# One matrix product over high and low activations together, in the feed-forward layers of a two-block transformer kernel

## The chip, the cores and the metric

The kernel runs on one core of one Trainium2 chip. The metric is the device time of one execution in microseconds (us): 1653.76 us, the median of three runs (1652.23 to 1656.18).

TensorE (PE in the profile) multiplies matrices and writes to PSUM, which here is two tensors of four banks, `psw` and `psa`, each bank 128 partitions x 512 fp32 values. VectorE (DVE), ScalarE (ACT) and GpSimd (POOL) work on SBUF and PSUM; SyncE (SP) issues the loads. Each engine runs its own instruction list in order, and waits on semaphores for the others.

## The reference

Two blocks, each of two layers (`L = 2`), act on 256 tokens of width 1024 in fp32. What bears on the change are the four feed-forward layers, with an inner width of 2816. Block 1:

```python
g, u = jnp.split(x @ w_gu, 2, axis=-1)
ffn = (jax.nn.silu(g) * u) @ w_down
ple = (p_i @ w_pp) * jax.nn.sigmoid(x @ w_pg)
return layer_norm(DN_ALPHA * x + ffn + ple, ln2_g, ln2_b)
```

Block 2 puts a causal convolution of three taps over the tokens between the product and the gate:

```python
u = x @ w_up
u = lax.conv_general_dilated(u, conv_w[:, None, :], padding=[(CONV_W - 1, 0)], ...) + conv_b
a, g = jnp.split(u, 2, axis=-1)
return (a * jax.nn.silu(g)) @ w_down
```

Around them stand the attentions, the norms and the other projections, which the change does not touch.

## The kernel before, in words

**Products in three parts.** TensorE takes fp32r operands here. To keep the precision of fp32, each weight tile (128 x 2048 values, 1 MB) is split: ScalarE rounds it to its high part `whi` (`split`, L1179), VectorE subtracts that from the original and has the low part `wlo` (L1515). Activations are split in the same way into `xhi` and `xlo`. `product` (L687) then adds three matrix products into one bank: high x high, high x low, low x high. Low x low is dropped.

**A feed-forward layer** is cut into `FS = 11` steps of 256 inner columns. A step has a gate tile `g` and an up tile `u` (`by_features`, L737: two halves of 128 features, in each 8 values of k, in each three matmuls over 256 tokens), then a down tile `d` of an earlier step (`down`, 24 matmuls of 512 columns into `psa`). `down_steps(s)` gives which: step s runs the down tile s-1 for s = 1 to 8, none in step 9, tile 8 in step 10, and behind the steps tiles 9 and 10 interleaved by token half and column half. The gate tile of a step fills bank 0 or 2 of `psw` and the up tile bank 1 or 3, alternately, so that two steps' results can stand at once.

**What follows a tile.** In block 1, ScalarE takes silu of the gate bank (L1380), and VectorE multiplies by the up bank (L1916), rounds (L1921) and subtracts (L1923): the two parts of `hidden(s)`, released by `hid_ready`. In block 2, ScalarE first makes the middle tap and the bias of the convolution from the bank (L1488, two instructions a tile), VectorE adds the other two taps (L2103, eight instructions a step), ScalarE takes silu (L1494), and VectorE multiplies (L2113), rounds (L2119) and subtracts (L2121).

**Order of the splits.** Weights move through rings: five raw tiles and five low tiles, three high tiles. `serve(key)` on ScalarE and VectorE issues the splits for which the tile `key` makes room; a high part can be made once the tile three places before it in the ring is done. So the tile done first makes room for one that is needed two tiles later. Where `serve` stands among the other instructions of ScalarE and VectorE sets which goes first. SP loads a raw tile when the tile five places before it is done.

**Block 1's per-layer gate.** The four banks of `x @ w_pg` go through exp (ScalarE, L1370) and, on VectorE, +1, reciprocal (L1898) and a product with `ple` (L1901), in the order of the loop at L1892. All of it stands ahead of step 0. TensorE waits for all four exps (`pg_exp`, L976) before step 0. In step 2 `ple` is added to `xtok` (L1933).

Of the kernel before, what the change touches and what calls it, by code (L numbers as in the profile page):

```python
# [9 lines left out]
F32R = mybir.dt.float32r  # L10
I32 = mybir.dt.int32
ALU = mybir.AluOpType
# [3 lines left out]
P = 128  # L16
# [188 lines left out]
def build(nc, w, c, out):  # L205
# [41 lines left out]
    with ExitStack() as ctx:  # L247
# [16 lines left out]
        xhi = sb("xhi", [KD, S], F32R)  # L264
        xlo = sb("xlo", [KD, S], F32R)
# [154 lines left out]
        xpT_ready = sem("xpT_ready")  # L420
        conv_first = sem("conv_first")
# [52 lines left out]
        conv_g = r1[:, 2560:3584].rearrange("p (b c s) -> p b c s", b=2, c=2)  # L474
        gact = r1[:, 512:1536].rearrange("p (b c) -> p b c", b=2)
# [205 lines left out]
        def _(pe):  # L681
# [67 lines left out]

            def norm_turns(key, t, src=xtok):  # L750
# [93 lines left out]
            def ffn(block, l, f0, norm_key, behind_up=lambda: None):  # L844
# [38 lines left out]
            for l in range(L):  # L883
# [92 lines left out]
                pe.wait_ge(pg_exp, 4 * (l + 1))  # L976

                def next_p():
                    pe.wait_ge(hid_ready, FS * (l + 1) - 1)
                    p_turns(l + 1, 2 * ((l + 1) * FS % 2))  # L980
                if l + 1 < L:
                    ffn(1, l, FS * l, None, next_p)
                else:
                    ffn(1, l, FS * l, None)
# [186 lines left out]
        def _(act):  # L1171
# [62 lines left out]

            def p_high(l, bank):
# [65 lines left out]
            for l in range(L):  # L1301
# [71 lines left out]
                for s in range(FS + 1):  # L1373
                    f = FS * l + s
                    if s < FS:
                        serve((1, "g", l, s))
                        if f >= 2:
                            act.wait_ge(hid_ready, f - 1)
                        act.wait_ge(tile_done, ti[(1, "g", l, s)] + 1)
                        nc.scalar.activation(gact[:, f % 2, :], psw[:, 2 * (f % 2), :],  # L1380
                                             ACT.Silu).then_inc(gate_ready, 1)
                        serve((1, "u", l, s))
                    if s == FS - 1 and l + 1 < L:
                        p_high(l + 1, 2 * ((l + 1) * FS % 2))
# [6 lines left out]
            for l in range(L):  # L1391
# [85 lines left out]
                for s in range(FS + 1):  # L1477
                    f = FS * (L + l) + s
                    if s < FS:
                        for name, buf, bank, ch0 in (("g", conv_g, 2 * (f % 2), 22 + 2 * s),  # L1480
# [748 lines left out]
```

## Time and profile before

| | |
|---|---|
| median of three runs | 1653.76 us |
| the profiled execution | 1651.49 us, its span 1649.7 us |
| PE busy | 1531.9 us (93%), 9781 matmuls |
| DVE busy | 1055.8 us (64%) |
| ACT busy | 716.0 us (43%) |
| mean granted TensorE clock | 0.966 of full |

Busy time of a matmul is a modelled duration, and neighbours overlap: how fast TensorE goes is read from the distance of the starts in a timeline. A group's mean duration is therefore longer than the time that one of its matmuls takes in a row of them. The idle time named in a group is that of its engine just before it, with what ended it. A wait for several semaphores is put down to the one that came last.

### The profile page before, as it was taken

To read this page: it belongs to the slowest core of one execution; us is meant where nothing else is said; L and a number is where in the kernel's file an instruction comes from. 1 tells how busy PE (TensorE), PEld (TensorE's weight loads), DVE (VectorE), ACT (ScalarE), POOL (GpSimd) and SP (SyncE) were. 2 spreads that over 40 slices of the span, in tenths; PEclk is the share of its full clock that TensorE was granted. 3 is DMA by queue.
4 is the path that set the end of the run, shared out by engine and by line. 5 is a ranking of instruction groups with operands and counts; after the bars stand their busy time and mean duration, and the time that the engine had idled before them with its cause. 6 is when DMAs were issued, how large, how long until landed. Compare 5 with 4: busy or idle time off the path is not lost.

```text
span 1649.7 us, 24186 instructions
## 1 busy us (share of the span) xinstructions
PE 1531.9 (93%) x9781; PEld 1365.4 (83%) x9781; DVE 1055.8 (64%) x1676; ACT 716.0 (43%) x1042; POOL 61.9 (4%) x58
## 2 busy tenths in 40 slices
PE   6799999999989999979999889999899998899997
PEld 5677899998777999968877769999788777799996
DVE  6786955567869664575365456677853664566766
ACT  4355333334553333424464343545444652435442
POOL 0100000000100000011000000000010000000000
PEclk9899999999999999989999999999999998899998
DMA  8533555655434655634433623556445346335551
GB/s 294 180 128 111 177 179 190 213 182 182 138 113 147 224 193 179 232 126 127 155 118 117 222 100 132 188 194 205 154 126 156 117 134 205 101 130 188 194 179 51
DMA packets 184690, 267.26 MB, mean 162 GB/s; under 512 B 7382, under 2 KB 139396, under 8 KB 184452
## 3 DMA queue, kind: packets, MB, share of 16 engines
q1 hardware_dynamic: 179684, 260.48, 47.9%
q10 hardware_dynamic: 4896, 5.25, 0.9%
q8 instruction: 78, 1.28, 0.3%
q14 instruction: 32, 0.26, 0.0%
HBM read 260.46 MB, written 5.24 MB: 161 GB/s over the span
## 4 chain that ended last, share of the span: by engine, by line
PE 71%; DVE 15%; ACT 4%; DVEq 4%; issue 3%; POOL 2%; DMA 1%; SPq 0%; ACTq 0%; POOLq 0%
PE psw L689 16%; PE psw L691 16%; PE psw L690 16%; PE psa L689 4%; PE psa L690 4%; PE psa L691 4%; DVE wlo L1515 3%; POOL rstd L2148 2%; PE psa L778 2%; PE psa L781 2%; DVE xtok L1547 1%; DVE sy L1603 1%; DVE r L1898 1%; DVEq L1607 1%; PE psw L799 1%
## 5 line engine op out<-in xcount | busy, mean ns | idle before, releaser
L1515 DVE TENSOR_TENSOR wlo<-raw,whi 128x2048 fp32r<-128x2048 f32 (+2 forms) x201 | 452.9, 2259 | 318.3 <-ACT whi L1179 318.0
L1179 ACT ACTIVATE whi<-raw 128x2048 fp32r<-128x2048 f32 (+2 forms) x201 | 379.5, 1890 | 338.6 <-PE psw L691 247.3
L689 PE MATMUL psw<-xhi,whi 128*128 128x256 f32 x1472 | 416.8, 283 | 2.6 <-ACT r L1370 1.4
L691 PE MATMUL psw<-xhi,wlo 128*128 128x256 f32 x1472 | 416.6, 283 | 0.0
L690 PE MATMUL psw<-xlo,whi 128*128 128x256 f32 x1472 | 416.5, 283 | 0.0
L689 PEld LDWEIGHTS psw<-xhi,whi 128*128 128x128 f32 x1472 | 282.4, 192 | 5.1 <-ACT r L1370 2.2
L690 PEld LDWEIGHTS psw<-xlo,whi 128*128 128x128 f32 x1472 | 282.4, 192 | 1.2
L691 PEld LDWEIGHTS psw<-xhi,wlo 128*128 128x128 f32 x1472 | 282.5, 192 | 0.0
L689 PE MATMUL psw<-whi,xhi 128*128 128x512 f32 (+3 forms) x472 | 184.9, 392 | 16.9 <-DVE wlo L1515 13.8
L691 PE MATMUL psw<-whi,xlo 128*128 128x512 f32 (+3 forms) x472 | 181.4, 384 | 0.0
L690 PE MATMUL psw<-wlo,xhi 128*128 128x512 f32 (+3 forms) x472 | 181.4, 384 | 0.0
L689 PE MATMUL psa<-whi,rr 128*128 128x512 f32 x352 | 139.1, 395 | 5.4 <-DVE wlo L1515 5.4
L690 PE MATMUL psa<-wlo,rr 128*128 128x512 f32 x352 | 138.4, 393 | 0.0
L691 PE MATMUL psa<-whi,rr 128*128 128x512 f32 x320 | 124.5, 389 | 0.0
L689 PEld LDWEIGHTS psw<-whi,xhi 128*128 128x128 f32 x472 | 90.8, 192 | 35.2 <-DVE wlo L1515 15.6
L1488 ACT ACTIVATE r<-psw,pcol 128x256 f32<-128x256 f32 x88 | 45.0, 562 | 146.0 <-PE psw L691 146.0
L2103 DVE SCALAR_TENSOR_TENSOR r<-psw,pcol,r 128x255 f32<-128x255 f32 (+1 forms) x176 | 72.8, 476 | 54.3 <-ACT r L1488 52.7
L691 PEld LDWEIGHTS psw<-whi,xlo 128*128 128x128 f32 x472 | 90.5, 192 | 16.3
L690 PEld LDWEIGHTS psw<-wlo,xhi 128*128 128x128 f32 x472 | 90.8, 192 | 15.3
L1267 ACT ACTIVATE sy<-sy,nmx 128x256 f32<-128x256 f32 (+1 forms) x160 | 70.6, 443 | 54.6 <-DVE nmx L1616 54.6
L2148 POOL TENSOR_TENSOR rstd<-vare,mhalf 128x1 f32<-128x1 f32 x26 | 38.6, 1484 | 1459.2 <-DVE vare L1537 1459.2
L689 PEld LDWEIGHTS psa<-whi,rr 128*128 128x128 f32 x352 | 67.0, 190 | 19.2 <-issue 6.2
(261 smaller groups left out, 1944.2 us busy)
## 6 DMA issues: line engine op xcount, KB each, us to landing
raw<-in_w_gu SPq DMA_DIRECT2D x44, 1024.0 KB, 5.1
raw<-in_ffn_w_up SPq DMA_DIRECT2D x42, 1024.0 KB, 5.1
raw<-in_w_down SPq DMA_DIRECT2D x22, 1024.0 KB, 4.9
raw<-in_ffn_w_down SPq DMA_DIRECT2D x22, 1024.0 KB, 4.9
raw<-in_w_in SPq DMA_DIRECT2D x20, 1024.0 KB, 5.4
raw<-in_xa_wkv SPq DMA_DIRECT2D x16, 1024.0 KB, 5.5
raw<-in_w_o SPq DMA_DIRECT2D x8, 1024.0 KB, 5.1
raw<-in_w_out SPq DMA_DIRECT2D x8, 1024.0 KB, 5.3
```

The costliest lines, as they stand in the source:

```text
L689: pe.matmul(o, lh, rh, start=first, stop=False)
L690: pe.matmul(o, lh, rl, start=False, stop=False)
L691: return pe.matmul(o, ll, rh, start=False, stop=last)
L778: ins = pe.matmul(psa[:, 3, 0:TC], weight[:, k, piece], memT[:, k, :], start=k == 0, stop=k == KD - 1)
L781: ins = pe.matmul(psa[:, 3, 0:TC], memT[:, k, piece], weight[:, k, :], start=k == 0, stop=k == KD - 1)
L799: ins = pe.matmul(psw[:, 2 * (i % 2) + a, b * S:b * S + nk], qT(kind, h, t), kT(kind, h, nk), start=True, stop=True)
L1179: nc.scalar.activation(tile_flat("hi", i), tile_flat("raw", i), ACT.Copy).then_inc(hi_ready, 1)
L1267: ins = nc.scalar.activation(soft[:, u % 2, h, 0:nk], soft[:, u % 2, h, 0:nk], ACT.Exp, bias=nmx[:, u % 2, h:h + 1], scale=1.0, accum_out= ...
L1488: ins = nc.scalar.activation(buf[:, f % 2, ch, :], bank2(psw, bank)[:, ch, :], ACT.Identity, scale=pcol[:, 2 + 2 * l, cc:cc + 1], bias=pco ...
L1515: v.tensor_tensor(tile_flat("lo", i), tile_flat("raw", i), tile_flat("hi", i).bitcast(F32), ALU.subtract).then_inc(lo_ready, 1)
L2103: ins = v.scalar_tensor_tensor(out=o, in0=bank2(psw, bank)[:, ch, 0:S - lag], scalar=pcol[:, j, cc:cc + 1], in1=o, op0=ALU.mult, op1=ALU.add)
L2148: g.tensor_tensor(rstd[:, t:t + 1], vare[:, t:t + 1], mhalf[:, t:t + 1], ALU.pow).then_inc(ln_rstd, 1)
```

## The change

Four things are done together.

1. `xhi` and `xlo` become the two halves of one buffer `xboth`. For the gate and up tiles `by_features_wide` replaces `by_features`: for each k, one matmul takes the high weights against both halves at once (512 columns: columns 0 to 255 of the bank get high x high, 256 to 511 high x low) and one takes the low weights against `xhi` (256 columns, into the first half). A half tile of 128 features now fills a whole bank; the gate tile uses banks 0 and 1, the up tile banks 2 and 3, in every step.
2. The two halves of a bank have to be added: `ffn_low` (ScalarE) copies the second halves to SBUF, `ffn_sum` (VectorE) adds the first halves and writes `gsum` or `usum` in SBUF. silu, the products and the convolution read these in place of PSUM. TensorE waits for `ffn_summed` of the step before, bank pair by bank pair, where it waited for `hid_ready` of two steps before.
3. VectorE's order: in block 2 the taps are made for the gate tile and the up tile apart; in both blocks the product and its rounding go ahead of the splits that the up tile releases. At the end of a feed-forward layer TensorE runs both column halves of down tile 9 and then both of tile 10, for each token half.
4. Block 1's gates (+1, reciprocal, product) are spread over steps 1 to 4, `ple` is added in step 5, and TensorE waits bank by bank for the exps.

```diff
-        xhi = sb("xhi", [KD, S], F32R)
-        xlo = sb("xlo", [KD, S], F32R)
+        xboth = sb("xboth", [2, KD, S], F32R)
+        xhi, xlo = xboth[:, 0], xboth[:, 1]
...
+            def by_features_wide(key, bank0, free, ready=None):
+                wh, wl = take(key)
+                for ch in range(TC // P):
+                    bank = psw[:, bank0 + ch, :]
+                    cols = slice(ch * P, (ch + 1) * P)
+                    free(bank0 + ch)
+                    for k in range(KD):
+                        if ready is not None and ch == 0:
+                            turns_ready(ready, NT - 1, k)
+                        if k:
+                            pe.matmul(bank[:, 0:S], wl[:, k, cols], xhi[:, k, :], start=False, stop=False)
+                        ins = pe.matmul(bank.rearrange("p (i s) -> p i s", i=2), wh[:, k, cols], xboth[:, :, k, :],
+                                        start=k == 0, stop=k == KD - 1)
+                        if k == 0:
+                            pe.matmul(bank[:, 0:S], wl[:, k, cols], xhi[:, k, :], start=False, stop=False)
+                ins.then_inc(tile_done, 1)
...
-                    if f >= 2:
-                        pe.wait_ge(hid_ready, f - 1)
-                    by_features((block, "g", l, s), bank2(psw, 2 * (f % 2)), xhi, xlo,
-                                norm_key if s == 0 else None)
-                    by_features((block, "u", l, s), bank2(psw, 2 * (f % 2) + 1), xhi, xlo)
+                    def gate_free(bank):
+                        if s:
+                            pe.wait_ge(ffn_summed, 2 * f - 1)
+                        else:
+                            first_free(bank)
+                    def up_free(bank):
+                        if s:
+                            pe.wait_ge(ffn_summed, 2 * f)
+                        else:
+                            first_free(bank)
+                    by_features_wide((block, "g", l, s), 0, gate_free, norm_key if s == 0 else None)
+                    by_features_wide((block, "u", l, s), 2, up_free)
...
                     for half in range(2):
                         ins = down(FS - 2, t, half)
-                        if t == 1 and half == 1:
-                            ins.then_inc(tile_done, 1)
+                    if t == 1:
+                        ins.then_inc(tile_done, 1)
+                    for half in range(2):
                         ins = down(FS - 1, t, half)
...
-                pe.wait_ge(pg_exp, 4 * (l + 1))
+                def gate_read(bank):
+                    pe.wait_ge(pg_exp, 4 * l + (1, 3, 2, 4)[bank])
...
+            def ffn_low(block, l, s, i):
+                act.wait_ge(tile_done, ti[(block, "gu"[i], l, s)] + 1)
+                nc.scalar.activation(low_part[:, i], psw[:, 2 * i:2 * i + 2, S:2 * S], ACT.Copy).then_inc(low_out, 1)
...
+            def ffn_sum(block, l, s, i):
+                dve.wait_ge(low_out, 2 * (FS * (l + L * (block - 1)) + s) + i + 1)
+                v.tensor_tensor((gsum, usum)[i].rearrange("p (c s) -> p c s", c=2), psw[:, 2 * i:2 * i + 2, 0:S],
+                                low_part[:, i], ALU.add).then_inc(ffn_summed, 1)
...
+                        ffn_sum(2, l, s, 0)
+                        taps(l, s, 0, conv_g, gsum, 22 + 2 * s).then_inc(conv_done, 1)
                         serve((2, "g", l, s))
-
-                        dve.wait_ge(conv_first, 2 * (FS * l + s + 1))
...
-                        if s < FS - 1:
-                            serve((2, "u", l, s))
+                        ffn_sum(2, l, s, 1)
+                        taps(l, s, 1, conv_a, usum, 2 * s)
                         dve.wait_ge(gate_ready, f + 1)
...
-                    if s == FS - 1:
+                    if s < FS:
                         serve((2, "u", l, s))
```

VectorE in one step of block 2's first layer (step 7 of 11), before. `r<-psw,pcol,r` are taps, `wlo` a split, `r<-r 128x512` the product, the two `rr` rows the two parts of the hidden tile.

```order
L2103 SCALAR_TENSOR_TENSOR r<-psw,pcol,r 128x255 x4
L2103 SCALAR_TENSOR_TENSOR r<-psw,pcol,r 128x254 x4
L1515 TENSOR_TENSOR wlo<-raw,whi 128x2048
L2113 TENSOR_TENSOR r<-r 128x512
L2119 CAST rr<-r 128x512
L2121 TENSOR_TENSOR rr<-r,rr 128x512
L1515 TENSOR_TENSOR wlo<-raw,whi 128x2048 x2
```

The same engine and step in the changed kernel (`r<-psw,r 128x512` is the sum of the two halves):

```order
L1725 TENSOR_TENSOR r<-psw,r 128x512
L2152 SCALAR_TENSOR_TENSOR r<-r,pcol 128x255 x2
L2152 SCALAR_TENSOR_TENSOR r<-r,pcol 128x254 x2
L1558 TENSOR_TENSOR wlo<-raw,whi 128x2048
L1725 TENSOR_TENSOR r<-psw,r 128x512
L2152 SCALAR_TENSOR_TENSOR r<-r,pcol 128x255 x2
L2152 SCALAR_TENSOR_TENSOR r<-r,pcol 128x254 x2
L2168 TENSOR_TENSOR r<-r 128x512
L2174 CAST rr<-r 128x512
L2176 TENSOR_TENSOR rr<-r,rr 128x512
L1558 TENSOR_TENSOR wlo<-raw,whi 128x2048 x2
```

The taps are in two groups, each behind a sum, the split of the up tile moved behind the hidden tile, and a step has two more instructions of 512 columns.

TensorE at the start of a tile in the changed kernel, first half of the features of block 1's first gate tile:

```order
L767 MATMUL psw<-xboth,whi 128x512
L770 MATMUL psw<-xboth,wlo 128x256
L766 MATMUL psw<-xboth,wlo 128x256
L767 MATMUL psw<-xboth,whi 128x512
L766 MATMUL psw<-xboth,wlo 128x256
L767 MATMUL psw<-xboth,whi 128x512
L766 MATMUL psw<-xboth,wlo 128x256
```

Where three matmuls of 256 columns stood for each k, one of 512 and one of 256 stand now.

## Rows read from the trace of the kernel before

**Rows 1.** The page, part 4: share of the span by line, largest first.

```profile
PE psw L689 16%; PE psw L691 16%; PE psw L690 16%; PE psa L689 4%; PE psa L690 4%; PE psa L691 4%; DVE wlo L1515 3%; POOL rstd L2148 2%; PE psa L778 2%; PE psa L781 2%; DVE xtok L1547 1%; DVE sy L1603 1%; DVE r L1898 1%; DVEq L1607 1%; PE psw L799 1%
```

**Rows 2.** Stretches: window, length, busy (instructions) of PE, PEld, DVE, ACT, POOL, clock, DMA.

```profile
200.00:350.00 150.00, 149.60 (x1075) 141.72 (x1074) 82.76 (x58) 57.13 (x37) 0.00 (x0) 1.00 0.57 189
1012.00:1164.00 152.00, 152.00 (x1097) 144.33 (x1096) 110.65 (x131) 76.68 (x76) 0.00 (x0) 1.00 0.59 199
...
1176.00:1180.00 4.00, 4.00 (x13) 3.15 (x13) 3.01 (x3) 0.00 (x0) 0.00 (x0) 0.68 0.02 9
```

**Rows 3.** Groups by form, PE: count, busy us, mean ns, idle before.

```profile
L689 PE MATMUL psw<-xhi,whi 128*128 128x256 f32 x1472 | 416.8, 283 | 2.6 <-ACT r L1370 1.4 <-DVE wlo L1515 1.2
...
L689 PE MATMUL psw<-xhi,ext 128*128 128x256 f32 x64 | 22.1, 346 | 2.6 <-DVE xlo L1562 2.6
```

**Rows 4.** Timeline of PE: start us, us, instruction; 42 starts between the first two.

```profile
234.88 0.28 PE L689 MATMUL psw<-xhi,whi 128*128 128x256 f32 x1
...
240.04 0.28 PE L690 MATMUL psw<-xlo,whi 128*128 128x256 f32 x1
...
172.15 0.40 PE L689 MATMUL psw<-whi,xhi 128*128 128x512 f32 x1
...
173.29 0.39 PE L691 MATMUL psw<-whi,xlo 128*128 128x512 f32 x1
```

**Rows 5.** Timeline of ACT, one step of block 2: idle before in brackets.

```profile
1063.88 1.02 ACT L1488 ACTIVATE r<-psw,pcol 128x256 f32<-128x256 f32 x2 [3.78 <-PE psw L691]
1064.80 1.91 ACT L1179 ACTIVATE whi<-raw 128x2048 fp32r<-128x2048 f32 x1
1069.64 1.02 ACT L1488 ACTIVATE r<-psw,pcol 128x256 f32<-128x256 f32 x2 [2.94 <-PE psw L691]
...
1080.87 1.02 ACT L1488 ACTIVATE r<-psw,pcol 128x256 f32<-128x256 f32 x2 [3.78 <-PE psw L691]
```

**Rows 6.** Timeline of DVE, the same step.

```profile
1070.70 3.38 DVE L2103 SCALAR_TENSOR_TENSOR r<-psw,pcol,r 128x255 f32<-128x255 f32 x8 [1.67 <-ACT r L1488]
1074.00 2.28 DVE L1515 TENSOR_TENSOR wlo<-raw,whi 128x2048 fp32r<-128x2048 f32 x1
1076.38 0.69 DVE L2113 TENSOR_TENSOR r<-r 128x512 f32<-128x512 f32 x1
1077.14 0.43 DVE L2119 CAST rr<-r 128x512 fp32r<-128x512 f32 x1
1077.64 0.69 DVE L2121 TENSOR_TENSOR rr<-r,rr 128x512 fp32r<-128x512 f32 x1
1078.25 2.29 DVE L1515 TENSOR_TENSOR wlo<-raw,whi 128x2048 fp32r<-128x2048 f32 x1
```

**Rows 7.** Groups by form, ACT and DVE: kinds of instruction that the change adds or turns.

```profile
L1197 ACT ACTIVATE xhi<-psa 128x512 fp32r<-128x512 f32 x40 | 22.6, 598 | 75.0 <-PE psa L756 74.9
...
L1562 DVE TENSOR_TENSOR xlo<-psa,xhi 128x512 fp32r<-128x512 f32 x40 | 26.1, 685 | 9.9 <-ACT xhi L1197 9.7
...
L1267 ACT ACTIVATE sy<-sy,nmx 128x256 f32<-128x256 f32 x80 | 39.6, 496 | 30.2 <-DVE nmx L1616 30.2
...
L1468 ACT ACTIVATE sy<-psw,xmx 128x256 f32<-128x256 f32 x16 | 7.4, 473 | 10.1 <-DVE xmx L2083 10.1
...
L1796 DVE SCALAR_TENSOR_TENSOR r<-sy,wi_s,r 128x256 f32<-128x256 f32 x14 | 6.8, 484 | 1.0
```

**Rows 8.** What PE waited for over the whole span: total us, times, longest.

```profile
PE psa L689 <- DVE wlo L1515: 5.4, 2, 2.7
...
PE psw L689 <- ACT r L1370: 1.4, 2, 0.7
```

**Rows 9.** Timeline of PE: block 1's waits at step 1, both layers.

```profile
200.82 0.39 PE L689 MATMUL psw<-xhi,whi 128*128 128x256 f32 x1 [0.40 <-DVE wlo L1515]
...
545.95 0.36 PE L689 MATMUL psw<-xhi,whi 128*128 128x256 f32 x1 [0.84 <-DVE wlo L1515]
```

**Rows 10.** Timeline of DVE: one gate's reciprocal of block 1, and the splits behind it.

```profile
194.44 3.35 DVE L1898 RECIPROCAL r<-r 128x512 f32<-128x512 f32 x1
...
198.48 6.69 DVE L1515 TENSOR_TENSOR wlo<-raw,whi 128x2048 fp32r<-128x2048 f32 x3
```

More of the change, by code:

```diff
@@ L842, in attention, with ffn @@
                                 ins.then_inc(pt_done, 1)
-            def ffn(block, l, f0, norm_key, behind_up=lambda: None):
+            def ffn(block, l, f0, norm_key, behind_up=lambda: None, first_free=lambda bank: None):
                 def down(j, t, half):
@@ L1479, in _ @@
                     if s < FS:
-                        for name, buf, bank, ch0 in (("g", conv_g, 2 * (f % 2), 22 + 2 * s),
-                                                     ("u", conv_a, 2 * (f % 2) + 1, 2 * s)):
-                            act.wait_ge(tile_done, ti[(2, name, l, s)] + 1)
+                        for i, (name, buf, whole, ch0) in enumerate((("g", conv_g, gsum, 22 + 2 * s),
+                                                                     ("u", conv_a, usum, 2 * s))):
+                            ffn_low(2, l, s, i)
                             if f >= 2:
                                 act.wait_ge(hid_ready, f - 1)
+                            act.wait_ge(ffn_summed, 2 * f + i + 1)
                             for ch in range(2):
                                 cc = ch0 + ch
-                                ins = nc.scalar.activation(buf[:, f % 2, ch, :], bank2(psw, bank)[:, ch, :],
+                                ins = nc.scalar.activation(buf[:, f % 2, ch, :], whole[:, ch * S:(ch + 1) * S],
                                                            ACT.Identity, scale=pcol[:, 2 + 2 * l, cc:cc + 1],
@@ L1890, in _, with gated @@
                 residual_norm(1, "o", l, (1, "1", l), False, (1, "pg", l, 0))
-                for j, (q, t) in enumerate(((1, 0), (1, 1), (3, 0), (3, 1))):
-                    g = q // 2
+                for q in range(4):
+                    serve((1, "pg", l, q))
+                def gated(j):
+                    g, t = divmod(j, 2)
                     dve.wait_ge(pg_exp, 4 * l + j + 1)
@@ L1901, in _ @@
                     v.tensor_tensor(ple[:, t, cols], ple[:, t, cols], e, ALU.mult)
-                    if j == 1:
-                        for done in range(3):
-                            serve((1, "pg", l, done))
-                    if j == 3:
-                        serve((1, "pg", l, 3))
                 for s in range(FS + 1):
@@ L1930, in _ @@
                             serve((1, "d", l, j))
-                    if s == 2:
+                    if s == 5:
+                        dve.drain()
                         for t in range(NT):
@@ L2090, in _, with taps @@
                 residual_norm(2, "xo", l, (2, "2", l), True, (2, "g", l, 0))
+                def taps(l, s, i, buf, whole, ch0):
+                    f = FS * (L + l) + s
+                    dve.wait_ge(conv_first, 2 * (FS * l + s) + i + 1)
+                    for tap, lag in ((1, 1), (0, 2)):
+                        for ch in range(2):
+                            cc = 44 * tap + ch0 + ch
+                            o = buf[:, f % 2, ch, lag:S]
+                            ins = v.scalar_tensor_tensor(out=o, in0=whole[:, ch * S:(ch + 1) * S - lag],
+                                                         scalar=pcol[:, 1 + 2 * l, cc:cc + 1], in1=o, op0=ALU.mult,
+                                                         op1=ALU.add)
+                        if tap:
+                            dve.drain()
+                    return ins
                 for s in range(FS + 1):
```

54 lines of the change are left out of this document (26 added, 28 removed).

## The prediction

> **What bounds the kernel now.** I read the chain of waits first. TensorE's products hold most of it, the three matmuls into `psw` with 16% of the span each [rows 1]; the gate and up tiles are 507 us of it (4224 matmuls of 120 ns, both numbers worked out below). Then the stretches inside the feed-forward layers: in block 1 TensorE is busy for 149.60 of 150 us, in block 2 for 152.00 of 152, at the full clock, while VectorE is busy 55% and 73% of the time [rows 2]. So inside these layers TensorE alone sets the pace, and work on the other two engines costs nothing until it makes TensorE wait. Third, the timeline, for TensorE's real pace, since the mean of 283 ns in the groups is a modelled one that overlaps: from 234.88 to 240.04 stand 43 distances in 5.16 us, 120.0 ns for each matmul of 256 columns. From 172.15 to 173.29 stand five distances of 512 columns, 228 ns each [rows 4]. The difference, 108 ns for 256 columns, is 0.42 ns a column, which is the 2.4 GHz level; of the 120 ns some 13 do not depend on the width. That fixed part is what the change can save: it makes two matmuls of three.
>
> **1. The wide matmul.** The groups have 1472 + 64 products of this form [rows 3]; 128 of them are the cross attention's queries (2 layers x 4 tiles x 16), which stay, so 1408 are changed (44 steps x 2 tiles x 16). A step before takes 1080.87 - 1063.88 = 16.99 us, of which a tile takes 1069.64 - 1063.88 = 5.76 us = 48 x 120 ns [rows 5]; the rest, 5.47 us, is the down tile, 24 x 228 ns. A product costs 360 ns before. After, it costs 120 + 227.5 ns, 347.5 ns: with starts given to 0.01 us the 228 may be 226 to 230, and I take a value in its lower half. The saving is 12.5 ns x 1408 = 17.6 us, 4.4 us in each of the four layers, and a step takes 16.59 us. No row shows a moving operand that lies in two pieces, as `xboth[:, :, k, :]` does. It could cost all of the 12.5 ns (then the matmul takes what two narrow ones do), or it could be a little cheaper: half of the 13 ns fixed part again, 6.5 ns, is my lower end, 9 us over all products. I take no extra cost, since each piece is a row of 256 values as before, and fill and load of a matmul are the same.
>
> The Trainium skill (TensorE: Matmul & The Clock Gate, Back-to-back issue gap) has N/2.4 + 2.5 ns for a full-clock matmul. By that, three narrow take 327.5 ns and the new pair 325.0, a saving of 2.5 ns a product, an estimate of 3.5 us in all. The trace differs: 120.0 ns where the rule gives 109.2 [rows 4].
>
> **2. Steady steps of block 2: is VectorE still on time?** Of a step's 16.59 us VectorE now needs the following. Two sums: the nearest row is a subtraction with one PSUM operand, 685 ns, of which the next instruction waits 0.59 as in the pair at 1077.64 and 1078.25 [rows 6, 7]: 1.18. Behind each sum it waits for ScalarE's two first taps: 1.02 us as before [rows 5], plus 0.03 for reading SBUF, plus the tail of the sum and two handovers, some 1.23 each: 2.46. Taps: 0.415 us each (3.30 us from the first tap to the split, for eight), plus a drain in each group, 1.77 and 1.89: 3.66. Product 0.76, rounding 0.50, subtraction 0.61, taken from start to start: 1.87. Three splits of 2.20: 6.60. With 0.04 for handover this is 15.8 us. It leaves 0.8 us a step. The splits still come in time. After the end of an up tile, ScalarE's copy and the handovers take some 1.2 us, then come sum 0.59, wait 1.23, taps 1.89, hidden tile 1.87, split 2.20: the next up tile's low part is there after 9.0 us, and TensorE takes it after 5.47 + 5.56 = 11.0. So TensorE stays the bound, but VectorE's idle time, 27% before, has shrunk to 0.8 us a step beside its waits for ScalarE. ScalarE: two copies more (598 ns each [rows 7]), some 9.9 of 16.6 us, no bound. In step 1, which has no down tile ahead of it, VectorE is behind and the up tile of step 2 waits about 0.3 us: +0.3 per layer of block 2.
>
> What the source of the taps costs is shown near enough: a tap-like instruction from SBUF over 256 columns takes 484 ns [rows 7], against 476 as the taps' mean before. ScalarE's exp over 256 columns takes 496 ns from SBUF and 473 from PSUM [rows 7]. The Trainium skill (VectorE: DVE Perf Modes, The TRN2 errata) has 224 against 172 fixed cycles for ScalarE and 58 against 120 for VectorE. The sign for ScalarE agrees with the rows, 23 ns against its 43; for VectorE the rows show no gain. It moves the sum by less than 0.3 us a step either way.
>
> **3. End of block 2's layers.** Before, TensorE waits 2.7 us in each for the low part of down tile 10 [rows 8]. After, VectorE is behind here, since steps 9 and 10 follow each other without a down tile. From the end of gate tile 9 TensorE needs three tiles (16.7), down tile 8 (5.5) and now both halves of tile 9 (2.7): 24.9 us. VectorE starts on gate tile 9 about 1.1 us after its end (last layer) or 2.5 us (first layer, where a split of the next stage's extra tile stands ahead), and needs 2 x 13.6 us (a step as above with two splits): 28.3 and 29.7. The wait becomes 3.4 and 4.8 us. Against the 2.7 or 2.8 of before that is +0.6 and +2.0. Down tile 9's second half, run ahead of the wait, is already in the 24.9. The clock fell to 0.68 behind this wait [rows 2]; a longer wait may cost another 0 to 2 us, in the range.
>
> So block 2 gains 4.4 - 0.3 - 2.0 = 2.1 and 4.4 - 0.3 - 0.6 = 3.5 us, 5.6 in all.
>
> **4. Block 1.** No convolution: VectorE needs 1.2 for sums, 1.9 for the hidden tile, 6.6 for splits, 9.7 us, and in steps 1 to 4 4.5 us for a gate (reciprocal 3.35 [rows 10], the +1, the product, starts 4.5 apart): 14.2 of 16.6 us. It fits; the split that waits behind the gate is that of a down tile which is needed some 5 us later. So 4.4 us in each layer, 8.8. The gates of before kept the low parts late: TensorE waited 0.40 and 0.84 us at step 1 [rows 9], with three splits in a row behind the last gate [rows 10]. These 1.2 us go. So does the wait of 0.7 us for the last exp, twice [rows 8]: bank 0 has been read long before. Together 2.6 us. What is late next at the start is nothing: gate tile 1's low part is due at 199 us and can be made at 193. Moving the addition of `ple` to step 5 (2.35 us) lies in idle time.
>
> **5. The new bank wait.** Before, TensorE could write two steps ahead. Now the gate tile of step s waits for the sum of s-1. That one ends 1.5 us after its tile, and TensorE is back at this bank pair after the up tile and a down tile, 11 us (5.6 where there is none). Behind this wait on TensorE stand all its later matmuls, but it is met. Cost 0. It only bites if VectorE is more than 4 us behind.
>
> **Sum.** 8.8 + 2.6 + 5.6 = 17.0 us off. The profiled execution took 1651.5 us (span 1649.7 and 1.8 around it), so 1634.5. The median shown is 2.3 us above the profiled time, which gives 1636.8. I say 1636.
>
> **Rivals.**
>
> A. *VectorE becomes the bound in block 2: slower.* Place: each of the steps 2 to 9 of the two layers. It decides from the 0.8 us of slack on. If a sum over two banks, or a handover, costs 0.9 us more than my rows say, a step has 1.8 us more, 1.0 over TensorE's. By the same addition TensorE waits about 3 us in step 2, 1.0 in each of seven more, and some 4 more at the end. Against before block 2 loses 13 and 11 us instead of gaining 5.6. With block 1's 11.4 us off that is +13, 1664 us. At 0.6 us a sum it comes out even, at about 1651 to 1654. For it: 95% load, six handovers in each step in series where there were three. Against: each price has a near row, and walking the step of before with such prices gives VectorE's idle 1.67 us and the last wait of 2.7.
>
> B. *The wide matmul is hardly cheaper.* If the second piece brings a fixed part of its own, of the size that a second matmul has (13 ns), or of four fifths of it, the 17.6 us shrink to between 0 and 3.5. What remains are the 2.6 us at the start of block 1, less about 1 lost at the end of block 2: 1646 to 1650 by the profiled time, up to 1652 by the median. The rule of the Trainium skill cited in part 1 would end here too, at 1646 to 1647. For it: no row with two pieces. Against: 228 ns for 512 columns in one piece.
>
> C. *More than forecast*: 226 ns for 512 columns and no extra wait at the ends of block 2. 20 + 2.6 = 22.6, less 0.3: 1629 to 1631.
>
> **How the numbers follow.** Forecast with its own spread (1630.5 to 1641.5): 0.71. B: 0.09. A in its even form: 0.07, in its slower form: 0.07. C: 0.06. A kernel like this is told from no change by about 0.2%, 3.3 us. Faster: 0.71 + 0.06 + two thirds of B = 0.83. Same: a third of B and the even form of A = 0.10. Slower: 0.07. Range: 1630 to 1648. The lower end takes in most of C, the upper end half of B and a mild A; beyond it lie some 12%, and 4% below.
>
> **What the profile after would show.** Starts of 0.347 us a pair in the gate and up tiles, without a gap between half tiles (else B). Idle of TensorE before a `psw` matmul released by VectorE `wlo` in the middle steps of block 2: 0.3 us at one step (else A). The wait at down tile 10 with 3.4 and 4.8 us. No wait for the exps and none at step 1 of block 1. VectorE's step of block 2 with 0.8 us of idle before the gate's sum, over the handover. I am wrong if the pair takes over 355 ns, or if in block 2 the steps are longer than 16.7 us.

## The result and the profile after

The changed kernel takes 1644.18 us (median of 4 runs, 1642.2 to 1644.53) against 1654.97 for the kernel before in the same comparison: a ratio of 0.9940, with a 95% interval of 0.9928 to 0.9951. So it is faster, by 10 to 11 us (10.8 by the medians) where 17 were forecast, and lies in the range, but 8 us above the predicted 1636.

From the page of the profile: the shares, the clock row and some groups. TensorE has 1408 matmuls fewer; VectorE's share has risen.

```profile
span 1642.7 us, 21591 instructions
PE 1524.8 (93%) x8373; PEld 1292.6 (79%) x8373; DVE 1115.7 (68%) x1764; ACT 767.1 (47%) x1130; POOL 61.8 (4%) x58
PEclk9999999999999999989899889999998998989999
L767 PE MATMUL psw<-xboth,whi 128*128 128x512 f32 x1376 | 475.5, 396 | 0.6 <-DVE wlo L1558 0.6
L766 PE MATMUL psw<-xboth,wlo 128*128 128x256 f32 x1204 | 335.7, 279 | 0.0
L1273 ACT ACTIVATE r<-psw 128x512 f32<-128x512 f32 x88 | 52.7, 598 | 213.0 <-PE psw L767 212.9
L1725 DVE TENSOR_TENSOR r<-psw,r 128x512 f32<-128x512 f32 x88 | 60.6, 688 | 64.7 <-ACT r L1273 64.7
```

The same kind of stretches as in [rows 2], and the two ends of block 2's layers, from the last product of up tile 10 to the last start of a down tile. Columns: window, length, busy (instructions) of PE, PEld, DVE, ACT, POOL, clock, DMA share, GB/s.

```profile
200.00:350.00 150.00, 150.00 (x803) 128.82 (x802) 113.26 (x92) 67.39 (x57) 0.00 (x0) 1.00 0.58 195
1002.00:1154.00 152.00, 151.71 (x812) 130.04 (x810) 123.98 (x151) 86.44 (x92) 0.00 (x0) 1.00 0.60 203
1153.95:1178.79 24.84, 19.68 (x75) 15.37 (x73) 19.22 (x27) 8.72 (x9) 1.52 (x1) 0.86 0.32 94
1611.39:1633.22 21.83, 18.24 (x74) 14.57 (x73) 16.09 (x24) 5.80 (x6) 1.52 (x1) 0.92 0.00 0
```

Inside the layers TensorE still sets the pace (one idle time of 0.29 us in block 2's 152). VectorE is busy 82% of that stretch, where it was 73% before, and beside this it waits for ScalarE. The same ends in the kernel before:

```profile
1165.74:1186.37 20.63, 17.91 (x74) 14.44 (x73) 15.18 (x23) 5.38 (x5) 1.52 (x1) 0.92 0.33 102
1619.39:1640.17 20.78, 18.06 (x75) 14.53 (x73) 12.98 (x22) 3.46 (x4) 1.52 (x1) 0.92 0.00 1
```

The timeline of TensorE in a gate or up tile: start, modelled duration, instruction. It answers to [rows 4].

```profile
233.57 0.28 PE L766 MATMUL psw<-xboth,wlo 128*128 128x256 f32 x1
233.69 0.40 PE L767 MATMUL psw<-xboth,whi 128*128 128x512 f32 x1
233.93 0.28 PE L766 MATMUL psw<-xboth,wlo 128*128 128x256 f32 x1
234.05 0.40 PE L767 MATMUL psw<-xboth,whi 128*128 128x512 f32 x1
234.28 0.28 PE L766 MATMUL psw<-xboth,wlo 128*128 128x256 f32 x1
```

Narrow to wide is 0.12 us, wide to narrow 0.23 to 0.24: a pair takes 0.35 us. What TensorE waited for, the lines that answer to [rows 8], and the wait at down tile 10 of the first layer with what stands behind it:

```profile
PE psa L694 <- DVE wlo L1558: 8.8, 3, 4.9
PE psw L767 <- DVE wlo L1558: 0.6, 2, 0.3
```

```profile
1162.67 0.39 PE L696 MATMUL psa<-whi,rr 128*128 128x512 f32 x1
1167.99 0.77 PE L694 MATMUL psa<-whi,rr 128*128 128x512 f32 x1 [4.93 <-DVE wlo L1558]
1168.56 0.63 PE L695 MATMUL psa<-wlo,rr 128*128 128x512 f32 x1
1168.98 0.63 PE L696 MATMUL psa<-whi,plo 128*128 128x512 f32 x1
1169.41 0.63 PE L694 MATMUL psa<-whi,rr 128*128 128x512 f32 x1
```

Behind the wait the starts are 0.43 us apart where they were 0.23: the granted clock is 0.50 from 1168 to 1170 us, its lower level, 1.2 GHz. The waits of block 1's starts ([rows 8, 9]: 0.7 twice, 0.40, 0.84) are gone.

The layers, from TensorE's timeline (us; block 1 from the transposes ahead of the layer, block 2 from its first product, each to the last start of the down tiles):

| | before | after | change |
|---|---|---|---|
| block 1, first layer | 207.83 | 202.39 | -5.44 |
| block 1, last layer | 207.80 | 201.95 | -5.85 |
| block 2, first layer | 192.74 | 193.92 | +1.18 |
| block 2, last layer | 193.15 | 190.95 | -2.20 |
| all the rest of the span | 848.2 | 853.5 | +5.3 |

The forecast had 11.4 us off in block 1 (it is 11.3) and 5.6 in block 2 (it is 1.0). In the rest no instruction was changed.

### The profile page after: what moved, and what is told of

It is laid out like the page before. It is cut to its first block, busy times and chain, and to the rows that moved or that the text cites. A ratio compares the mean times of both kernels' runs of the same rounds, so it can differ in the third digit from the quotient of the medians.

```text
span 1642.7 us, 21591 instructions
## 1 busy us (share of the span) xinstructions
PE 1524.8 (93%) x8373; PEld 1292.6 (79%) x8373; DVE 1115.7 (68%) x1764; ACT 767.1 (47%) x1130; POOL 61.8 (4%) x58
## 4 chain that ended last, share of the span: by engine, by line
PE 69%; DVE 16%; ACT 5%; DVEq 4%; issue 4%; POOL 2%; DMA 1%; SPq 0%; ACTq 0%; POOLq 0%
PE psw L767 17%; PE psw L766 7%; PE psw L694 7%; PE psw L695 7%; PE psw L696 7%; DVE wlo L1558 5%; PE psa L694 4%; PE psa L695 4%; PE psa L696 4%; POOL rstd L2203 2%; PE psa L804 2%; PE psa L801 2%; DVE xtok L1590 1%; PE psw L822 1%; DVE sy L1646 1%
## 5 line engine op out<-in xcount | busy, mean ns | idle before, releaser
L767 PE MATMUL psw<-xboth,whi 128*128 128x512 f32 x1376 | 475.5, 396 | 0.6 <-DVE wlo L1558 0.6
L766 PE MATMUL psw<-xboth,wlo 128*128 128x256 f32 x1204 | 335.7, 279 | 0.0
L767 PEld LDWEIGHTS psw<-xboth,whi 128*128 128x128 f32 x1376 | 248.4, 188 | 49.2 <-DVE wlo L1558 1.2
L766 PEld LDWEIGHTS psw<-xboth,wlo 128*128 128x128 f32 x1204 | 227.0, 189 | 7.7
L694 PE MATMUL psw<-whi,xboth 128*128 128x512 f32 (+3 forms) x472 | 184.0, 390 | 17.2 <-DVE wlo L1558 15.0
L695 PE MATMUL psw<-wlo,xboth 128*128 128x512 f32 (+3 forms) x472 | 181.0, 383 | 0.0
L696 PE MATMUL psw<-whi,xboth 128*128 128x512 f32 (+3 forms) x472 | 180.6, 383 | 0.0
L694 PEld LDWEIGHTS psw<-whi,xboth 128*128 128x128 f32 x472 | 90.2, 191 | 35.4 <-DVE wlo L1558 16.7
L2152 DVE SCALAR_TENSOR_TENSOR r<-r,pcol 128x254 f32<-128x254 f32 (+1 forms) x176 | 77.3, 481 | 57.8 <-ACT r L1530 53.8
L1725 DVE TENSOR_TENSOR r<-psw,r 128x512 f32<-128x512 f32 x88 | 60.6, 688 | 64.7 <-ACT r L1273 64.7
L696 PEld LDWEIGHTS psw<-whi,xboth 128*128 128x128 f32 x472 | 90.2, 191 | 16.2
L695 PEld LDWEIGHTS psw<-wlo,xboth 128*128 128x128 f32 x472 | 90.2, 191 | 15.2
```

The source lines that it names most:

```text
L694: pe.matmul(o, lh, rh, start=first, stop=False)
L695: pe.matmul(o, lh, rl, start=False, stop=False)
L696: return pe.matmul(o, ll, rh, start=False, stop=last)
L766: pe.matmul(bank[:, 0:S], wl[:, k, cols], xhi[:, k, :], start=False, stop=False)
L767: ins = pe.matmul(bank.rearrange("p (i s) -> p i s", i=2), wh[:, k, cols], xboth[:, :, k, :], start=k == 0, stop=k == KD - 1)
L1725: v.tensor_tensor((gsum, usum)[i].rearrange("p (c s) -> p c s", c=2), psw[:, 2 * i:2 * i + 2, 0:S], low_part[:, i], ALU.add).then_inc(ffn_ ...
```

## The experiments

All times are medians. The edits are shown in short, with `...` or a comment where lines are left out. The kernel before, run beside each group of kernels, took 1653.73, 1653.71 and 1653.87 us.

**Does the operand in two pieces cost anything?** `one_piece` gives the wide matmul an operand whose 512 columns lie in one row (it then multiplies other values).

```diff
-   wh[:, k, cols], xboth[:, :, k, :],
+   wh[:, k, cols], xboth[:, k % 2, 2 * (k // 2):2 * (k // 2) + 2, :],
```

> The changed kernel, but the 512 columns of the wide matmul are one contiguous piece of xboth (two neighbouring k of the high part for even k, of the low part for odd k) in place of a piece of the high and a piece of the low part: part of the products are other products, the count, widths and banks are the same. Theory P (the second piece costs 6 ns a matmul): the distance from a wide matmul to the next falls from 233.5 to about 227.5 ns, a step of block 1 from about 16.6 to 16.55 us (32 x 6 = 0.2 us less), four layers together 8 us less. Rival Q (the cost comes from a narrow matmul ahead, or the stamps shift between neighbours): the distances stay at 116 and 233.5 ns, a pair at 350 ns, and the time stays within noise of 1644.

Measured: 1640.14 us (one run, so the time itself tells little), pairs of 0.350 us, narrow to wide 0.116, wide to narrow 0.234, as in the changed kernel. Its feed-forward layers take 787.6 us together, the changed kernel's 789.2 in one profile and 788.6 in another. The second piece costs nothing that can be seen.

**Does it cost to go back and forth between widths?** `grouped` does the 8 wide matmuls of a half tile first, then the 8 narrow ones.

```diff
-   for k: narrow wl x xhi; wide wh x xboth      # in words
+   for k: wide wh x xboth
+   for k: narrow wl x xhi
```

> The changed kernel with the eight wide matmuls of a half tile first and then the eight narrow ones (same sums, another order). If the alternation of widths costs (Q), wide-wide distances are 227.5 and narrow-narrow 120, 347.5 ns a pair. If two pieces cost (P), wide-wide stays at 231 to 234 and a half tile takes at least 2.8 us. If neither, half a tile takes 2.78 us, against 2.79 to 2.80 in the changed kernel.

Measured: 1641.22 us (one run). Its timeline of TensorE (x8 is a row of eight):

```profile
233.52 1.12 PE L768 MATMUL psw<-xboth,wlo 128*128 128x256 f32 x8
234.47 2.00 PE L765 MATMUL psw<-xboth,whi 128*128 128x512 f32 x8
236.31 0.40 PE L768 MATMUL psw<-xboth,wlo 128*128 128x256 f32 x2
```

Eight narrow take 0.95 us, eight wide 1.84, a pair 0.349. Going back and forth costs at most 1 or 2 ns a pair. So 0.35 us is simply what one wide and one narrow matmul take.

**The gates and the earlier start alone.** `gates_only` is the kernel before with block 1's gates spread over steps 1 to 4, the addition in step 5, and the wait for the exps taken bank by bank.

```diff
-   pe.wait_ge(pg_exp, 4 * (l + 1))
+   pe.wait_ge(pg_exp, 4 * l + (1, 3, 2, 4)[bank])   # per bank, at its first use
-   the four gates in a row, ahead of step 0
+   if 1 <= s <= 4: gated(s - 1)                     # behind the hidden tile
```

> The kernel before, with the gates of block 1 spread over steps 1 to 4, the addition of ple in step 5 and the exps waited for bank by bank; nothing else of the change. My prediction gave this 2.6 us: ratio 0.9984, the waits of 0.69, 0.40, 0.69 and 0.84 us gone. A rival (the gates now delay the low parts of steps 1 to 4, since the old order of hidden tile behind the splits stands) gives 0 or a loss of up to 2 us.

Measured: 1651.61 us, ratio 0.9984, interval 0.9975 to 0.9993: 2.1 us. In its profile the two layers of block 1 are 1.6 and 2.0 us shorter, 3.6 where 2.6 were forecast. The forecast took the waits at their idle times: 0.69 us twice ahead of step 0, 0.40 and 0.84 at step 1. Without them the first product comes 0.84 and 0.82 us earlier, and the rest of the layer is another 0.77 and 1.16 us shorter. Idle time is counted from the modelled end of a matmul (0.28 us long), and in a row the next one starts after 0.12 us, so a wait costs more than its idle time shows, here by 0.1 to 0.4 us.

**The wide form in block 1 alone.** `block1_wide` is the changed kernel with the gate and up tiles, the convolution and the last down tiles of block 2 as before.

```diff
+   if block == 1:
        by_features_wide(...)
+   else:
+       by_features(..., xhi, xlo)        # three narrow products, as before
...
```

> The changed kernel in block 1, but block 2's feed-forward layers as before (narrow matmuls, banks, order, downs). By my prediction block 1 gives 8.8 + 2.6 = 11.4 us: ratio 0.993. By the trace after, block 1 gave 5.4 + 5.8 = 11.3 us and block 2 about +1.2 - 2.2 = -1, so a theory that block 2 gives nothing expects 0.9932, like the whole change (0.994). If block 2 did gain what I predicted (5.6 us), this kernel is 5 us slower than the changed one.

Measured: 1646.5 us, ratio 0.995, interval 0.9935 to 0.9964. Block 1's layers take 202.43 and 201.95 us, as in the changed kernel, so block 1 brings nearly all of the gain. Block 2's part would be the 2 or 3 us between this kernel's median and the changed one's, but the intervals of the two ratios overlap, and its layers take 191.02 and 194.07 us, together 0.2 us more than the changed kernel's: a gain in block 2 is not shown. Its waits for down tile 10 are those of before, 2.79 and 2.72 us, and yet its two ends differ by 2.8 us:

```profile
1157.45:1176.78 19.33, 16.54 (x75) 13.38 (x74) 15.09 (x23) 5.38 (x5) 1.52 (x1) 1.00 0.35 110
1614.56:1636.67 22.11, 19.39 (x74) 15.46 (x73) 12.97 (x21) 3.46 (x4) 1.52 (x1) 0.85 0.00 0
```

Behind the first wait the granted clock stayed at 1.00, behind the second it fell (0.50 from 1626 to 1630 us). What the clock costs behind a wait of this length thus differs from one wait to the next.

**The changed kernel again**, `after_again`, and what the rest of the span does.

> The changed kernel once more, unchanged. It tells how far the stages whose code is the same scatter from one execution to the next. If the 5 us by which these stages were longer in the profile of the changed kernel come from the draw of the granted clock, its stages between the feed-forward layers come out different by 1 to 3 us each with other clocks, and the median stays within 1642 to 1646.5. Rival: the changed kernel puts these stages into a colder state each time; then each of them repeats its length (167.0 us and 164.8 us for the two attention stages) within 0.5 us.

Measured: 1643.73 us, ratio 0.9941, interval 0.9928 to 0.9955. The two attention stages take 166.1 and 166.4 us, where they took 167.0 and 164.8: they don't repeat. I summed "all the rest of the span" for every profile: 848.2 us before, 853.5 and 850.9 for the two profiles of the changed kernel, 854.1 for `gates_only`, 856.7 for `block1_wide`, 848.9 to 854.6 for the others. The profile of before is the lowest of them all. Its execution was a favourable one (1651.49 us, medians 1653.7 to 1655.0), which accounts for 2 to 3.5 of the 5.3 us. Whether the remaining 2 to 3 us are real can't be settled with a scatter of 8 us.

**Is VectorE's slack in block 2 as small as it looks?** `sum_twice` does every sum twice.

```diff
+   for again in range(2):
        ins = v.tensor_tensor(gsum or usum, psw[...], low_part[:, i], ALU.add)
+       ...                                          # a drain between the two
```

> The changed kernel with every sum of the two accumulators done twice on VectorE, one behind the other: some 0.7 us more for each sum, 1.4 us a step. This is the prediction's rival A made on purpose. If a step of block 2 has 0.5 us of slack on VectorE, as the profile of the changed kernel shows, the steps 3 to 9 become 0.5 to 0.9 us longer, TensorE waits at their up tiles, and with the longer end a layer of block 2 costs 9 to 11 us more; block 1, where VectorE is idle 4 us or more a step, costs nothing. Time: 1662 to 1666 us, above the kernel before. Rival: VectorE has more room than that, because the splits may come late by half a tile's time without harm: only the end of each layer grows, by 2 x 1.4 us, and the time is 1650.

Measured: 1672.26 us, ratio 1.0114, interval 1.01 to 1.0128. Block 1 didn't move (202.43 and 201.92 us). Both layers of block 2 are 13.2 us longer or a little more. In the first, step 2's up tile waits 2.7 us, the two tiles of the steps 5 to 8 take 12.1 to 12.4 us, where they take 11.2 in the changed kernel, and its end takes 27.8 us:

```profile
PE psa L694 <- DVE wlo L1558: 15.4, 6, 5.7
PE psw L767 <- DVE wlo L1558: 12.6, 13, 2.7
```

In VectorE's timeline each tile's taps start 0.77 us later behind the first sum than in the changed kernel (2.68 us for 1.91), so a step has 1.5 us more work. With it VectorE is the bound, by 0.9 us a step. The slack is the difference, 0.6 us, near the 0.52 us of idle time in the changed kernel's step, and rival A was less than one sum's length away. The time ends above my 1662 to 1666; the granted clock is 0.90 around the wait in step 2 (1014 to 1031 us) and 0.88 in the first end, which the expectation left out.

**The order of the last down tiles.** `old_downs` takes pieces of tile 9 and 10 in turn, as the kernel before did.

```diff
    for half in range(2):
        ins = down(FS - 2, t, half)
-   for half in range(2):
        ins = down(FS - 1, t, half)
```

> The changed kernel, but the last two down tiles go in the order of the kernel before: for each group of tokens and each half, tile 9 and then tile 10. The wait for the low part of down tile 10 then stands ahead of three of the four pieces of tile 9 instead of two for the first token group. By the prediction's count one piece of tile 9 (1.37 us) then runs behind the wait instead of ahead of it: waits of 6.3 and 5.0 us in block 2, 1.4 us a layer, +2.8 us, 1647. In block 1 nothing waits there: 0. Rival: the order doesn't matter, since the norms behind it take the same pieces in any case (the first joined half is ready 1.4 us earlier with the old order): 1644 to 1645.

Measured: 1645.86 us, ratio 0.9956, interval 0.9944 to 0.9969, 2.1 us above the changed kernel beside it. The waits are 6.26 and 4.95 us, as expected: one piece of 1.37 us stands behind the wait instead of ahead of it.

**Whose wait is the one at down tile 10?** `narrow_last` gives the last step of block 2 its three narrow products back, so that step needs no copy and no sum; convolution reads PSUM there.

```diff
+   if block == 2 and s == FS - 1:
+       by_features((block, "g", l, s), bank2(psw, 0), xhi, xlo)
+       by_features((block, "u", l, s), bank2(psw, 2), xhi, xlo)
+   else:
        by_features_wide(...)
```

> The changed kernel, but the last step (10) of both feed-forward layers of block 2 has its gate and up tile as three narrow products, so that this step has no copy of the low part and no sum; its convolution reads PSUM. If VectorE's own work in steps 9 and 10 (the sums and the handovers to ScalarE around them) is what makes TensorE wait for down tile 10, this takes 2 x (0.59 us sum + 0.5 copy + 0.1 handover) off VectorE's chain and adds 2 x 0.17 us to TensorE: the waits of 4.9 and 3.6 us before down tile 10 shrink to about 0.6 and 0, and the time is 5 to 6.6 us below the changed kernel's, 1638 to 1639 us. Rival: the wait comes from something else (ScalarE's high part of down tile 10, or its DMA): waits stay at 4.9 and 3.6, time +0.7 us, 1645.

Measured: 1631.09 us, ratio 0.9861, interval 0.9848 to 0.9875: 12.6 us below the changed kernel, twice what I expected. Its two ends:

```profile
1152.50:1170.24 17.74, 16.52 (x74) 13.39 (x73) 16.55 (x23) 5.27 (x5) 1.52 (x1) 1.00 0.44 131
1600.13:1616.38 16.25, 16.25 (x75) 13.47 (x73) 12.92 (x19) 2.98 (x4) 1.52 (x1) 1.00 0.00 0
```

```profile
1160.58 0.39 PE L702 MATMUL psa<-whi,rr 128*128 128x512 f32 x1
1162.19 0.47 PE L700 MATMUL psa<-whi,rr 128*128 128x512 f32 x1 [1.22 <-DVE wlo L1575]
1162.50 0.39 PE L701 MATMUL psa<-wlo,rr 128*128 128x512 f32 x1
```

The waits are 1.22 and 0, near the 0.6 and 0 expected: VectorE's own work is what TensorE waits for. VectorE's timeline shows a larger relief than the 2.4 us expected: from the split ahead of each of the two tiles to the first tap it takes 2.20 us where it took 4.11, so 3.8 us in all. The ends are shorter by 7.1 and 5.6 us, of which the waits are 3.9 (4.93 + 0.23 - 1.22) and 3.6. The other 5.2 us are for the most part a thing that the expectation left out: the clock stays at 1.00 where it was 0.86 and 0.92. Some 0.3 us for each of the two waits that are gone belong to the waits themselves: here the one wait of 1.22 us makes its end 1.50 us longer than one without a wait, at the full clock.

**Is that really the clock?** `warm_end` leaves VectorE as late as it was and fills the waits with matmuls whose result nobody reads.

```diff
+   if block == 2 and t == 0:
+       pe.wait_ge(ffn_summed, 2 * (f0 + FS) - 1)
+       for _ in range((17, 12)[l]):
+           pe.matmul(psw[:, 0, :], hidden(FS - 2)[0][:, 0:P], wh[:, 0, 0:512], start=True, stop=True)
    ...
```

> The changed kernel, but TensorE fills most of its wait for down tile 10 in block 2 with matmuls whose result nobody reads: 17 of 512 columns in the first layer (3.9 us of the wait of 4.9), 12 in the last one (2.7 of 3.6). Nothing is made earlier. In the changed kernel the stretch from the last product of the up tile to the last one of the down tiles takes 24.8 and 21.8 us, against 16.3 us of work without a wait: the waits of 4.9 and 3.6 explain 21.2 and 19.9, the other 3.6 and 1.9 us would be the price of the clock that falls behind the wait. If so, here the stretches take 21.4 and 20.0 us and the time falls by about 5 us, to 1639. Rival: the matmuls behind the wait are slow for another reason (they wait for VectorE or for their weights in small pieces): stretches and time stay as in the changed kernel, 1644.

Measured: 1637.81 us, ratio 0.9900, interval 0.9884 to 0.9917: 5.9 to 6.4 us below the changed kernel, with useless work added. Its end in the first layer, by window and by timeline:

```profile
1150.69:1172.76 22.07, 20.81 (x92) 16.55 (x91) 18.44 (x26) 8.73 (x9) 1.52 (x1) 1.00 0.36 105
```

```profile
1159.40 0.39 PE L696 MATMUL psa<-whi,rr 128*128 128x512 f32 x1
1159.62 4.01 PE L914 MATMUL psw<-whi,rr 128*128 128x512 f32 x17
1164.70 0.47 PE L694 MATMUL psa<-whi,rr 128*128 128x512 f32 x1 [1.06 <-DVE wlo L1563]
1165.01 0.39 PE L695 MATMUL psa<-wlo,rr 128*128 128x512 f32 x1
```

Down tile 10 starts 5.30 us after the last start of down tile 9 before it, as in the changed kernel (5.32), but behind it the starts are 0.23 apart and the clock is 1.00. The ends take 22.07 and 20.15 us against 24.84 and 21.83: 4.4 us by the clock alone; the rest of the 6 us lies outside the ends and within their scatter.

**One narrow step more.** `narrow_two` has steps 9 and 10 narrow, each of their four tiles in a bank of its own.

> As the kernel with the last step of block 2's layers narrow, but steps 9 and 10 both. VectorE's chain is 2.4 us shorter again. Left to win are the last wait of 1.2 us in the first layer and the clock behind it (0.3); the narrow step costs TensorE 0.34 us a layer. Expected: -0.4 to -1.2 us in the first layer, +0.3 in the last, together 1630 to 1631, not told from the kernel with one narrow step. Rival: the start of the norm behind it comes earlier too, since VectorE is ahead there, and it gains 2 us or more, below 1629.

Measured: 1627.5 us (4 runs, 1625.5 to 1633.72), ratio 0.9846, interval 0.9824 to 0.9867. No wait is left at either end:

```profile
1152.64:1168.88 16.24, 16.24 (x74) 13.45 (x73) 13.38 (x18) 4.75 (x4) 1.52 (x1) 1.00 0.48 142
```

16.24 us is what these tiles take when nothing waits. Block 2's layers take 185.8 and 186.2 us, against 187.0 and 185.1 with one narrow step: 0.1 us less in both together, where 0.1 to 0.9 were expected. The median lies below the 1629 us that the rival named, and 3.6 us below that of `narrow_last`. But the rival's cause isn't there: from the last down start to the next matmul it is 0.23 us in the first layer, and to the end of the span 9.52 us in the last one, in both kernels. The intervals of the two ratios overlap too, so I don't count the difference as shown. Either of the two beats the changed kernel by 12 us or more, and the kernel before by 22 or more.

Steps 9 and 10 have the products of the kernel before again, and that kernel waits 2.72 us at each end. What still differs there is the order of VectorE's work and of the down tiles, of which `old_downs` prices the latter at 1.4 us a layer. Whether these orders alone would free the kernel before of its wait was not run.

## Why the prediction was right and where it fell short

**The mechanism** was right: TensorE sets the pace inside the layers, its tiles got shorter, VectorE stayed just in time, and the time fell. The 8 us between 1636.0 and the measured 1644.2 come from parts 1 and 3, from the starts of block 2's layers and from the base of the sum, less what part 4 brought more; a rest of 1.4 to 2.6 us stays open.

**Part 1, the pair of matmuls.** I took 347.5 ns from the lower half of 226 to 230 for 512 columns; it is 349 to 350, the upper end. A step of block 2 takes 16.63 us instead of 16.99, not 16.59. Comparing the first products to the last ones, `gates_only` against the changed kernel, the wide form brings 3.8 us in each layer of block 1 (186.96 to 183.13 and 186.51 to 182.67) where I had 4.4, so it is some 2.2 us short over four layers if block 2 is alike. The two bounds I kept (a second piece costs the fixed part; a piece is cheaper still) are both refuted by `one_piece`: 0.350 us a pair with either operand. Rival B is out.

The pair also shows where the fixed part is paid. The Trainium skill (TensorE: Matmul & The Clock Gate, Wait — 56ns, not 53.3ns?) says that a matmul's fixed cost shows only at the full clock, while at half clock the distance is N / 1.2 GHz. The trace agrees on the half clock: at block 2's start, with a granted clock of 0.50, a pair takes 0.64 us, and three narrow ones took 0.64 before:

```profile
986.28 0.41 PE L766 MATMUL psw<-xboth,ext 128*128 128x256 f32 x1
986.50 0.63 PE L767 MATMUL psw<-xboth,ext 128*128 128x512 f32 x1
986.92 0.41 PE L766 MATMUL psw<-xboth,ext 128*128 128x256 f32 x1
```

```profile
994.62 0.41 PE L690 MATMUL psw<-xlo,ext 128*128 128x256 f32 x1
994.83 0.41 PE L691 MATMUL psw<-xhi,ext 128*128 128x256 f32 x1
995.04 0.41 PE L689 MATMUL psw<-xhi,ext 128*128 128x256 f32 x1
995.26 0.41 PE L690 MATMUL psw<-xlo,ext 128*128 128x256 f32 x1
```

At the full clock the trace differs from it: by the page's figure the saving would be 2.5 ns a pair, an estimate; it is 10 to 11.

**Part 2, VectorE in block 2**, held in the main. The step in the changed kernel, VectorE's timeline, which answers to [rows 6]:

```profile
1061.03 0.68 DVE L1725 TENSOR_TENSOR r<-psw,r 128x512 f32<-128x512 f32 x1
1062.94 1.83 DVE L2152 SCALAR_TENSOR_TENSOR r<-r,pcol 128x255 f32<-128x255 f32 x4 [1.23 <-ACT r L1530]
1064.85 0.69 DVE L2168 TENSOR_TENSOR r<-r 128x512 f32<-128x512 f32 x1
1065.61 0.43 DVE L2174 CAST rr<-r 128x512 fp32r<-128x512 f32 x1
1066.11 0.69 DVE L2176 TENSOR_TENSOR rr<-r,rr 128x512 fp32r<-128x512 f32 x1
1066.72 4.49 DVE L1558 TENSOR_TENSOR wlo<-raw,whi 128x2048 fp32r<-128x2048 f32 x2
1071.73 0.69 DVE L1725 TENSOR_TENSOR r<-psw,r 128x512 f32<-128x512 f32 x1 [0.52 <-ACT r L1273]
```

The sum, the wait of 1.23 and the taps are those of the prediction within 0.1 us. The idle time is 0.52 us where I had 0.8, so VectorE's step is 16.1 us long, not 15.8. The wait at step 2's up tile is 0.29, as forecast, but it makes the tiles of that step 0.57 us longer (11.75 for 11.18), 0.5 us more than the sum had for both layers. Rival A did not happen, and `sum_twice` shows that it was a real one. Its 1664 us was added to the profiled 1651.5 without the 2.3 us that my own sum got; on the same footing it is some 1666.

**Part 3, the end of block 2's layers**, is the step that failed, though not in its waits. They are 4.93 and 3.59 us (4.8 and 3.4 forecast), with 0.23 in front of the first. What failed is "a longer wait may cost another 0 to 2 us, in the range": it was priced at zero in the sum. Against 16.24 us for an end in which nothing waits, the kernel before loses 4.4 and 4.5 us, 2.7 of it waiting, so 1.7 and 1.8 come behind the waits. The changed kernel loses 8.6 and 5.6, 5.2 and 3.6 of it waiting, and 3.4 and 2.0 come behind: 1.9 us more than before. Some 0.3 us of this comes with every wait even at the full clock (`narrow_last`, and the first end of `block1_wide`); the rest is the clock, about 1.6 us more than before. `warm_end` gives 4.4 of the 5.4 us back, and three times 0.3 is about what it leaves. How much the clock takes behind one wait also has luck in it: behind waits of 2.7 and 2.8 us it was, the 0.3 included, 1.7 and 1.8 us in the profile of before, 1.7 and 1.7 in that of `gates_only`, but 0.3 and 3.2 in that of `block1_wide`. The two profiles of the changed kernel agree within 0.2 us (24.84 and 24.62, 21.83 and 21.82). The larger oversight is one of reading: a wait that stood there before was taken as given, 2.7 us, when it cost 4.4 to 4.5, and `narrow_last` and `narrow_two` show that a wait at this place can be removed.

**Part 4, block 1**, came out at 11.3 us for 11.4 by luck, since two errors cancel: the wide form brought 7.7 instead of 8.8, the start 3.6 instead of 2.6, because I took waits at their idle times.

**Part 5, the new bank wait**, cost nothing, as said: no line of TensorE's waits names a sum as releaser. In `sum_twice` one does, with 0.9 us.

**The base.** The sum was made against an execution of 1651.5 us and corrected by 2.3 us from three runs. Over all comparisons before is at 1653.7 to 1655.0, and in that profile the untouched stages stood at the lower end of their scatter. That is why the profiles differ by 7 us when the medians differ by 10.8. Of the 8 us the base is 0 to 1.2, and my rounding from 1636.8 another 0.8.

**Added up:** 2.2 us for the pair; 2.7 for the ends (5.3 us longer where the sum had 2.6), of which some 1.6 are the clock; 0.5 for step 2; 0.4 for the starts of block 2's layers, where the clock is low and the wide form saves nothing; less 1.0 for block 1's start. That is 4.8 us, and the table of layers has 4.7 (12.3 us off for 17.0). Base and rounding add 0.8 to 2.0, which makes 5.6 to 6.8 of the 8.2. The other 1.4 to 2.6 us would lie in the stages whose code is unchanged and are left open: these scatter by 8 us over the profiles.

## What to carry to other kernels

A wait of a few us ahead of a row of matmuls costs its idle time and then more: some 0.3 us in any case, and often more because the granted clock falls behind it (both together, here: 1.7 us behind most waits of 2.7, but 0.3 and 3.2 behind two of them, 2.0 behind 3.6, 3.4 behind 5.2). Price both, and price the waits that are there already before you trade in tenths of a us elsewhere. When work is taken from the engine that bounds and given to one with a little slack, look at the ends of the loops, where there is no slack: undoing the trade in the last step alone (0.35 us more for TensorE, 3.8 off VectorE's chain) was worth 12.6 us in block 2's two layers, where the wide form saves TensorE 3.8 us a layer. Where untouched stages differ between two profiles, profile the same kernel twice before explaining it.

## What the runs showed of the hardware

- A moving operand of two rows of 256 columns costs what one of 512 does: 0.350 us a pair in either form.
- The saving by wider matmuls is there only at the full clock: 349 to 350 against 360 ns; at the lower level, a granted clock of 0.50, it is 0.64 against 0.64 us.
- A wait costs some 0.3 us more than its idle time even at the full clock: an idle time of 1.22 us made an end 1.50 us longer (`narrow_last`), one of 0.29 us a step's tiles 0.57 us longer (changed kernel).
- The granted clock doesn't fall behind every wait of the same length: in one profile (`block1_wide`) it was 1.00 behind 2.79 us and 0.50 behind 2.72 us.
- Matmuls whose result nobody reads made the kernel 6 us faster, by keeping the clock at 1.00 through waits of 4.9 and 3.6 us.
- Four taps of 255 and 254 columns take VectorE 1.83 us from SBUF (changed kernel) and 1.81 from PSUM (`narrow_last`): the source makes no difference to it here.
